# Low parts of the weights one use later, and a reordered projection stage in an NSA, S5 and mixed-attention kernel on one core

## The chip, the cores and the metric

One NeuronCore of a Trainium2 chip. The metric is the device time of one execution in microseconds (us), the median of the runs.

## The reference

A two-layer network on 512 tokens of width 1024, all in fp32. Layer 0 has a native-sparse-attention mixer and an S5 state-space mixer with a gated unit; the second block has a retention, a gated linear attention and a sliding-window attention, whose outputs are merged by gates; a feed-forward network ends it. Cut to what the change touches:

```python
def _compress(k, cmp_idx, pe, w1, w2):
    blk = k[:, cmp_idx] + pe[:, None, :]
    ...
    return jax.nn.silu(blk @ w1) @ w2

# mixer of layer 0: h @ w_in gives q, kc, vc, ks, vs, kw, vw, gates, z
k_cmp = _compress(kc, ...); v_cmp = _compress(vc, ...)      # 31 blocks of 32 tokens
s_c = einsum(q, k_cmp) - slopes * (t - cmp_center)
p_c = _masked_softmax(s_c, cmp_end <= t)                    # 16 heads
o = gate0 * (p_c @ v_cmp) + gate1 * selected + gate2 * window
# S5: state matrices from complex powers of 64-wide diagonals, applied in chunks
```

## The kernel before

The work is cut into tiles of 128 output columns by 512 tokens. Each fp32 product is three products of reduced-precision parts: hi times hi, hi times lo, lo times hi. So each weight piece (1024 columns by 128, 512 KB) goes through three steps: SyncE issues its load into one of 3 raw buffers, ScalarE copies it rounded to `whi` (L1249), VectorE subtracts to get `wlo` (L1720), both in a ring of 3. TensorE's `mm` (L822 to L824) uses one piece with the activations `Hh` and `Hl`, in 24 matmuls; `pair` (L842 to L844) runs two pieces side by side over the eight parts k of the activations, and waits for a piece's `wlo` at its first k and for `Hl` at each k, so that a norm still in the making paces it. `tok` (L861 to L863) has the weights move. There are 262 such pieces in the kernel.

The order is written once, by the class `Plan`: stages append steps to `self.order`, `with_weights` puts loads (`load`) and splits (`split`) in among them, and every engine walks the same list and does its own part of each step, in order. Waits are on semaphore counts. The piece that is `LOOK` = 2 uses ahead is split when a piece is first used. `tick()` puts a step of side work in between, which is `prep`: the state matrices of S5, made in the projection stage, in four rounds b. In each round `Bb` comes first, then the rotations CA (a power table `pw` times C, real and imaginary part) and W (`pr`, the table reversed, times `Bb`), six operations of half size each for one part; `prep_k` and `prep_wt` are matmuls that use them.

Before, VectorE does the real part of CA (`prep_ca`, 128x576), and POOL the imaginary one, its negation (`prep_neg`) and both parts of W. VectorE also makes the copies `Bd` of `Bb` (L1961) and, in `ev_kvc` (L1762), writes the tiles of w_kvc with the positional encoding added into `blk`. The compressed softmax (`cmp_soft`) works on a quarter of the queries and 16 heads after all eight score tiles. `Hl` is made at L1745 in the first norm, L1989 in the first block, L2326 before the feed-forward network; `total` (L874) sums squares over partitions.

The projection stage is `nsa`: squares of x, first norm, w_kvc in two pairs, the gate tile, cmp_w1 and cmp_out with tiles of w_q, six more tiles of w_q with scores, w_ksw with softmax, w_vsw, then the attention. `evict` gives a finished tile to the engine that copies it out.

```python
                if k == 0:
                    on.wait_ge(*before(plan.bank, key))
                    on.wait_ge(*at("wlo", i))
                on.wait_ge(*at("lo", src, k))
```

## Time and profile before

| | |
|---|---|
| median of 3 runs | 2047.48 us (2042.81 to 2052.18) |
| the profiled execution | 2053.18 us |
| its span, first to last instruction | 2051.4 us |
| TensorE busy | 1826.9 us, 89% |
| VectorE, ScalarE, POOL busy | 1005.5, 816.8, 303.3 us |
| mean granted clock of TensorE | 0.955 |

The span is cut by stage in what follows: 0 to 281 us the projection stage (with the S5 preparation), to 461 the attention, then the output projection w_o0, the S5 part, w_glu and w_o1, the second block from about 820 us, and the feed-forward network from 1640 us on. The granted clock is a share of full speed. Idle time in brackets names what ended it.

### The profile page before, as it was taken

The page shows a single profiled execution, that of the slowest core. Times are in us where ns is not written, and L with a number is a line of the kernel's source. Part 1 is how long each engine was busy: PE and PEld are TensorE (multiplying, and loading weights), DVE is VectorE, ACT ScalarE, POOL GpSimd, SP SyncE. Part 2 cuts the span into 40 slices and gives each one's busy share as a digit, 9 for nine tenths or more (in the row PEclk, how much of TensorE's full clock was granted, in tenths as well). Part 3 has the DMA queues.
Part 4 walks back from the last instruction along what each step waited for, and adds up shares of the span by engine and source line. Part 5 has one row for each costly group of instructions (what it writes and reads, how often), then busy time and mean ns, then how long its engine had stood idle before and what let it go on. Part 6 is the DMA issues. An engine that isn't in the chain of part 4 may idle for free.

```text
span 2051.4 us, 23580 instructions
## 1 busy us (share of the span) xinstructions
PE 1826.9 (89%) x9454; PEld 1450.1 (71%) x9454; DVE 1005.5 (49%) x1694; ACT 816.8 (40%) x1348; POOL 303.3 (15%) x376
## 2 busy tenths in 40 slices
PE   3488699997996999999799999999999969999996
PEld 2366578775775787786487777887777748888885
DVE  7647845665564446434434454445544364334323
ACT  4034356763313424333425545256632443223222
POOL 1347432546000000000000000012200021111000
PEclk9789799998998999999999999999999979999998
DMA  3154231005667422321032221321122212233231
GB/s 108 47 168 144 99 98 42 12 1 157 156 157 167 132 84 92 105 95 48 21 116 78 82 83 62 100 69 61 63 82 92 83 41 93 92 103 100 85 95 59
DMA packets 79230, 183.37 MB, mean 89 GB/s; under 512 B 24449, under 2 KB 35585, under 8 KB 77329
## 3 DMA queue, kind: packets, MB, share of 16 engines
q1 hardware_dynamic: 79120, 181.87, 28.7%
q8 instruction: 74, 1.21, 0.3%
q14 instruction: 36, 0.29, 0.0%
HBM read 165.58 MB, written 16.25 MB: 89 GB/s over the span
## 4 chain that ended last, share of the span: by engine, by line
PE 66%; DVE 17%; ACT 8%; DMA 4%; issue 2%; POOL 2%; SPq 1%; DVEq 0%; ACTq 0%; POOLq 0%
PE bank L822 16%; PE bank L823 16%; PE bank L824 15%; DVE wlo L1720 2%; PE bank L861 2%; PE bank L862 2%; PE bank L863 2%; PE bank L1003 2%; PE bank L981 2%; ACT whi L1249 1%; POOL Ps L2473 1%; ACT Ps L1619 1%; DVE Pb L1842 1%; DVE CA L1688 1%; PE bank L842 1%
## 5 line engine op out<-in xcount | busy, mean ns | idle before, releaser
L1720 DVE TENSOR_TENSOR wlo<-wraw,whi 128x1024 fp32r<-128x1024 f32 (+1 forms) x262 | 327.5, 1253 | 344.1 <-ACT whi L1249 342.7
L822 PE MATMUL bank<-Hh,whi 128*128 128x512 f32 (+2 forms) x1136 | 461.2, 406 | 24.0 <-DVE wlo L1720 13.2
L823 PE MATMUL bank<-Hl,whi 128*128 128x512 f32 (+2 forms) x1136 | 448.6, 395 | 0.0
L824 PE MATMUL bank<-Hh,wlo 128*128 128x512 f32 (+2 forms) x1136 | 448.2, 395 | 0.0
L1249 ACT ACTIVATE whi<-wraw 128x1024 fp32r<-128x1024 f32 (+1 forms) x262 | 271.1, 1040 | 373.0 <-PE bank L824 260.1
L822 PEld LDWEIGHTS bank<-Hh,whi 128*128 128x128 f32 (+2 forms) x1136 | 215.5, 190 | 84.5 <-DVE qs L1786 11.8
L824 PEld LDWEIGHTS bank<-Hh,wlo 128*128 128x128 f32 (+2 forms) x1136 | 215.3, 189 | 48.9 <-issue 0.6
L823 PEld LDWEIGHTS bank<-Hl,whi 128*128 128x128 f32 (+2 forms) x1136 | 215.8, 190 | 47.5 <-issue 2.7
L2466 POOL TENSOR_SCALAR bs<-dist 128x256 f32<-128x256 f32 x16 | 7.3, 457 | 831.8 <-DMA dist<-in_c_dist 831.1
L822 PE MATMUL bank<-Bh,whi 128*128 128x512 f32 x256 | 103.1, 403 | 2.2 <-DVE Bl L2244 2.2
L824 PE MATMUL bank<-Bh,wlo 128*128 128x512 f32 x256 | 102.1, 399 | 0.0
L823 PE MATMUL bank<-Bl,whi 128*128 128x512 f32 x256 | 101.9, 398 | 0.0
L1381 ACT ACTIVATE Pb<-Pb,stp 128x128 f32<-128x128 f32 (+3 forms) x128 | 70.8, 554 | 42.3 <-DVE stp L1842 41.5
L2428 POOL TENSOR_SCALAR Pb<-Pb,stp 128x128 f32<-128x128 f32 (+3 forms) x128 | 65.7, 532 | 100.7 <-DVE stp L1688 100.7
L1842 DVE CUSTOM_DVE_ANT_0 Pb<-bank,bias 128x128 f32<-128x128 f32 (+3 forms) x128 | 57.4, 487 | 33.1 <-PE bank L972 14.6
L842 PE MATMUL bank<-Hh,whi 128*128 128x512 f32 x80 | 36.3, 454 | 41.3 <-DVE Hl L2326 16.0
L861 PE MATMUL bank<-whi,Hh 128*128 128x512 f32 (+1 forms) x192 | 73.1, 381 | 0.0
L862 PE MATMUL bank<-whi,Hl 128*128 128x512 f32 (+1 forms) x192 | 72.6, 378 | 0.0
L863 PE MATMUL bank<-wlo,Hh 128*128 128x512 f32 (+1 forms) x192 | 72.5, 378 | 0.0
L822 PE MATMUL bank<-Fh,whi 128*128 128x512 f32 x176 | 69.8, 396 | 0.0
L823 PE MATMUL bank<-Fl,whi 128*128 128x512 f32 x176 | 69.8, 396 | 0.0
L824 PE MATMUL bank<-Fh,wlo 128*128 128x512 f32 x176 | 69.8, 396 | 0.0
(368 smaller groups left out, 3044.7 us busy)
## 6 DMA issues: line engine op xcount, KB each, us to landing
wraw<-in_w_o SPq DMA_DIRECT2D x24, 512.0 KB, 3.5
wraw<-in_w_bgate SPq DMA_DIRECT2D x24, 512.0 KB, 3.4
wraw<-in_w_branch SPq DMA_DIRECT2D x24, 512.0 KB, 3.5
wraw<-in_w_fg SPq DMA_DIRECT2D x22, 512.0 KB, 3.4
wraw<-in_w_fu SPq DMA_DIRECT2D x22, 512.0 KB, 3.4
wraw<-in_w_s SPq DMA_DIRECT2D x16, 512.0 KB, 4.1
wraw<-in_w_glu SPq DMA_DIRECT2D x16, 512.0 KB, 3.6
wraw<-in_w_fd SPq DMA_DIRECT2D x16, 512.0 KB, 3.5
```

Source lines behind the costliest of these rows:

```text
L822: pe.matmul(o, wh[:, cols], hi(k), start=k == 0, stop=False)
L823: pe.matmul(o, wh[:, cols], lo(k), start=False, stop=False)
L824: m = pe.matmul(o, wl[:, cols], hi(k), start=False, stop=k == K - 1)
L842: pe.matmul(o, wh[:, cols], hi(k), start=k == 0, stop=False)
L861: pe.matmul(o, hi(k)[:, rows], wh[:, cols], start=k == 0, stop=False)
L862: pe.matmul(o, lo(k)[:, rows], wh[:, cols], start=False, stop=False)
L863: m = pe.matmul(o, hi(k)[:, rows], wl[:, cols], start=False, stop=k == KT - 1)
L1249: return act.activation(o, i, ACT.Copy, **k)
L1381: x = act.activation(P[:, br, 0:W], P[:, br, 0:W], ACT.Exp, scale=-1.0, bias=s[:, n + br:n + br + 1], accum_out=s[:, 4 + n + br:5 + n + br])
L1720: dve.tensor_tensor(c.wlo[q][:, 0:n], c.raw[i % RR][:, 0:n], c.whi[q][:, 0:n].bitcast(F32), S_).then_inc(*up(DID, ("wlo", i)))
L1842: dve.tensor_tensor_reduce(out=P[:, br, 0:W], in0=bank(("s", u, m))[:, col:col + W], in1=bs[:, 512 - W:512], scale=1.0, scalar=3.0e38, op0 ...
L2428: gp.tensor_scalar(P[:, br, 0:W], P[:, br, 0:W], s[:, n:n + 1], 1.0, M, M).then_inc(*up(DID, ("pn", u + a, br)))
```

## The change

It does these things.

- In `with_weights` the high part stays where it was, two uses ahead. The low part becomes a step of its own, `split_lo`, and is put in at the first use of a piece: first the low part of the next piece, then the loads and the high part two ahead, then (if still open) its own. The raw buffer is free only after it. This holds for all 262 pieces of the kernel.
- The first norm: the table's small operations stand between the squares, the reciprocal root comes before the first three splits, and `norm0` makes `sq` of piece k+1 before `Hl` of k; low parts 0 to 2 come after all of it.
- The rotations run whole (128x1152, 128x1024) on VectorE, both parts, with the negation inside the last operation. POOL has only memsets and small copies in the stage.
- `Bd` copies and the tiles of w_kvc (`ev_kvc`) go to ScalarE; the positional encoding comes in as column 31 of `blk` and as a bias `hb` of the Silu.
- The compressed softmax runs per head index r (`soft_in`, `soft_out`), needs two score tiles, and has its mask in the bias and in `valid`.
- New tile order: one pair, then w_kvc 2 and 3 singly, gate, w_ksw with two cmp_w1 steps each, w_q in the order 0, 4, 1, 5, 2, 6, 3, 7, w_vsw. The stores of CA, K and W stand later. The wait for the last W store moves from POOL's `cmp_end` to ScalarE's first copies of the attention.

The core of the diff:

```diff
+        lows = deque()
+
+        def low(upto):
+            while lows and lows[0] <= upto:
+                i = lows.popleft()
+                out.append(("split_lo", i))
+                rawuser[i % RR] = -1
...
-                        rawuser[split % RR] = -1
+                        lows.append(split)
...
                     if i > seen:
                         seen = i
+                        low(i + 1)
                         pump(i + LOOK)
+                        low(i)
...
-            if k == 3:
-                self.tick(2)
+            if 1 <= k <= 6:
+                self.tick()
         self.step("consts")
         self.step("nsa_in")
+        self.inv("x", 0, 7, 0, 1.0 / D, "rs")
+        self.tick()
         self.step("pump")
-        self.inv("x", 0, 7, 0, 1.0 / D, "rs")
-        self.tick(3)
...
+        for n in range(2, 4):
+            self.filled("w_kvc", n, 3)
+        self.filled("w_gate", 0, 3, M=48)
         for t in range(4):
-            self.filled("w_ksw", t)
...
+            for hf in range(2):
+                j = self.piece("cmp_w1", (i, m, hf), 0, 1024, split=False)
+                self.step("cmp_w1", i, m, hf, j)
+                self.tick()
...
+        for n, t in enumerate(self.turns):
+            self.filled("w_q", t, 1)
+            if n == 0:
+                self.cmp_out(1)
+            self.compressed(n)
...
+    def rotated(o, x, w, n, y, i, b, step, *names):
...
+        if step == 0:
+            tt(o, yk(0), wk(i), M)
+        elif step == 1:
+            tt(x, yk(1), wk(1 - i), M)
+        else:
+            tt(o, o, x, A_ if i else S_, *names)
...
+        if (i, n) == (1, 2):
+            on.wait_ge(*now(DID))
+            dve.scalar_tensor_tensor(o, o, -1.0, x, M, S_).then_inc(*up(DID, ("CA", b)))
...
-    def prep_ca(b, n):
-        if n == 0:
-            on.wait_ge(*at("Cq", b))
-            on.wait_ge(*at("Bb", b))
...
-        rot(*c.rotate(c.tG, c.pw, 9, c.Cq, 1, c.CA[:, 1, :, :, :], b, n), *([("CA_im", b)] if n == 5 else []))
```

How the instructions stand, at three places. In the rows a name with a number is a buffer of a ring (wlo_57 to wlo_59 are the three low parts, wraw and whi the raw and high parts, sqb squares, nacc their sum).

VectorE before the w_s5 pair, in the kernel before; the pair uses wlo_58 and wlo_59:

```order
L1729 TENSOR_TENSOR nacc_67<-nacc_67,sqb_65 128x512
L1720 TENSOR_TENSOR wlo_59<-wraw_52,whi_56 128x1024
L1983 TENSOR_TENSOR X<-X,bank 128x512
L1989 SCALAR_TENSOR_TENSOR Hl<-X,vecs,Hh 128x512
L1729 TENSOR_TENSOR nacc_67<-nacc_67,sqb_66 128x512
L1994 TENSOR_TENSOR vecs<-vecs 128x8
L1995 MEMSET D_142 128x8
L1997 MEMSET Xs_151 128x16
L1997 MEMSET Xs_152 128x16
L1720 TENSOR_TENSOR wlo_57<-wraw_53,whi_54 128x1024
```

and with the change:

```order
L1769 TENSOR_TENSOR wlo_58<-wraw_51,whi_55 128x1024
L2029 TENSOR_TENSOR X<-X,bank 128x512
L2035 SCALAR_TENSOR_TENSOR Hl<-X,vecs,Hh 128x512
L1778 TENSOR_TENSOR nacc_67<-nacc_67,sqb_66 128x512
L2040 TENSOR_TENSOR vecs<-vecs 128x8
L2041 MEMSET D_140 128x8
L2043 MEMSET Xs_149 128x16
L2043 MEMSET Xs_150 128x16
L1769 TENSOR_TENSOR wlo_59<-wraw_52,whi_56 128x1024
L1769 TENSOR_TENSOR wlo_57<-wraw_53,whi_54 128x1024
```

The low part of the pair's second piece, wlo_59, stood eight rows higher, before the last tile's X, Hl and nacc; it stands behind them, beside that of the following piece.

VectorE before the w_fg/w_fu pair, whose norm is the rows X and Hl (ft and Fl are the feed-forward network's activations), before:

```order
L2315 SCALAR_TENSOR_TENSOR mg<-mg,vecs,rs 128x512
L2321 TENSOR_TENSOR X<-X,mg 128x512
L2326 SCALAR_TENSOR_TENSOR Hl<-X,vecs,Hh 128x512
L2321 TENSOR_TENSOR X<-X,mg 128x512
L2326 SCALAR_TENSOR_TENSOR Hl<-X,vecs,Hh 128x512
L1720 TENSOR_TENSOR wlo_58<-wraw_51,whi_55 128x1024
L2338 TENSOR_TENSOR ft_215<-bank,rs 128x512
L2341 TENSOR_TENSOR ft_215<-ft_215,bank 128x512
L2343 TENSOR_TENSOR Fl<-ft_215,Fh 128x512
L1720 TENSOR_TENSOR wlo_59<-wraw_52,whi_56 128x1024
```

and with the change:

```order
L2361 SCALAR_TENSOR_TENSOR mg<-mg,vecs,rs 128x512
L2367 TENSOR_TENSOR X<-X,mg 128x512
L2372 SCALAR_TENSOR_TENSOR Hl<-X,vecs,Hh 128x512
L2367 TENSOR_TENSOR X<-X,mg 128x512
L2372 SCALAR_TENSOR_TENSOR Hl<-X,vecs,Hh 128x512
L1769 TENSOR_TENSOR wlo_57<-wraw_53,whi_54 128x1024
L1769 TENSOR_TENSOR wlo_58<-wraw_51,whi_55 128x1024
L2384 TENSOR_TENSOR ft_213<-bank,rs 128x512
L2387 TENSOR_TENSOR ft_213<-ft_213,bank 128x512
L2389 TENSOR_TENSOR Fl<-ft_213,Fh 128x512
L1769 TENSOR_TENSOR wlo_59<-wraw_52,whi_56 128x1024
L1769 TENSOR_TENSOR wlo_57<-wraw_53,whi_54 128x1024
```

The pair's second low part is wlo_57, behind the last Hl; before, it stood ahead of the norm's first row.

VectorE in the first norm, around the first three low parts; before:

```order
L1729 TENSOR_TENSOR nacc_67<-nacc_67,sqb_65 128x512
L1733 MEMSET ones 128x128
L1734 MEMSET epst 128x1
L1735 MEMSET epst 128x1
L1720 TENSOR_TENSOR wlo_57<-wraw_51,whi_54 128x1024
L1720 TENSOR_TENSOR wlo_58<-wraw_52,whi_55 128x1024
L1720 TENSOR_TENSOR wlo_59<-wraw_53,whi_56 128x1024
L1688 TENSOR_TENSOR sm<-pw 128x32 x2
L1688 TENSOR_TENSOR pw<-sm 128x32
L1688 TENSOR_TENSOR sm<-pw 128x32 x2
```

and with the change:

```order
L1797 TENSOR_TENSOR Hl<-sq_64,Hh 128x512
L1792 SCALAR_TENSOR_TENSOR sq_64<-X,vecs,rs 128x512
L1797 TENSOR_TENSOR Hl<-sq_63,Hh 128x512
L1797 TENSOR_TENSOR Hl<-sq_64,Hh 128x512
L1769 TENSOR_TENSOR wlo_57<-wraw_51,whi_54 128x1024
L1769 TENSOR_TENSOR wlo_58<-wraw_52,whi_55 128x1024
L1769 TENSOR_TENSOR wlo_59<-wraw_53,whi_56 128x1024
```

They stood right behind the squares; they stand behind the last Hl, and before Hl the next piece's `sq` has its place.

## Rows read from the trace of the kernel before

**Rows 1.** the page, part 1, busy time of each engine

```profile
PE 1826.9 (89%) x9454; PEld 1450.1 (71%) x9454; DVE 1005.5 (49%) x1694; ACT 816.8 (40%) x1348; POOL 303.3 (15%) x376
```

**Rows 2.** windows of core 0 (columns: us, then each engine's busy us, clock, DMA share, GB/s)

```profile
0.00:281.00 281.00, 185.46 (x933) 146.12 (x934) 181.72 (x310) 91.44 (x141) 117.78 (x86) 0.87 0.35 116
281.00:461.00 180.00, 172.76 (x1355) 135.59 (x1355) 109.58 (x390) 123.53 (x336) 74.96 (x144) 0.99 0.08 25
461.00:2051.00 1590.00, 1468.63 (x7174) 1168.38 (x7170) 714.25 (x994) 601.85 (x871) 110.54 (x147) 0.97 0.30 92
...
220.00:240.00 20.00, 8.72 (x43) 7.20 (x43) 18.50 (x24) 7.11 (x12) 17.02 (x13) 0.76 0.18 53
```

**Rows 3.** waits of TensorE: us in total, times, longest

```profile
PE bank L822 <- DVE wlo L1720: 30.4, 7, 15.3
PE bank L905 <- DMA wraw<-in_cmp_w: 21.1, 1, 21.1
PE bank L1040 <- DMA mW<-scratch_W: 20.0, 2, 15.5
PE bank L842 <- DVE Hl L2326: 16.0, 7, 6.4
PE bank L951 <- DVE sC L1688: 15.3, 2, 11.3
PE bank L842 <- DVE wlo L1720: 13.6, 1, 13.6
```

**Rows 4.** timeline, start of the norm, first pair, attention (start us, us, instruction, [idle before])

```profile
28.65 0.74 DVE L1743 SCALAR_TENSOR_TENSOR sq<-X,vecs,rs 128x512 f32<-128x512 f32 x1
28.88 0.77 PE L842 MATMUL bank<-Hh,whi 128*128 128x512 f32 x1 [10.21 <-DVE Hl L1745]
...
30.10 0.69 DVE L1745 TENSOR_TENSOR Hl<-sq,Hh 128x512 fp32r<-128x512 f32 x1 [0.70 <-ACT Hh L1249]
...
281.20 0.29 DVE L1842 CUSTOM_DVE_ANT_0 Pb<-bank,bias 128x128 f32<-128x128 f32 x1 [7.28 <-POOL bias L2417]
```

**Rows 5.** groups of VectorE by line, 0 to 281 us

```profile
L1720 DVE TENSOR_TENSOR wlo<-wraw,whi 128x1024 fp32r<-128x1024 f32 (+1 forms) x23 | 34.8, 1524 | 34.9 <-ACT whi L1249 34.8
L1961 DVE COPY Bd<-Bb 64x128 f32<-64x128 f32 x16 | 16.7, 1043 | 0.3
```

**Rows 6.** timeline of VectorE, rotations beside POOL and without it

```profile
92.77 1.58 DVE L1688 TENSOR_TENSOR CA<-Cq,pw 128x576 f32<-128x576 f32 x1
...
242.31 0.76 DVE L1688 TENSOR_TENSOR CA<-Cq,pw 128x576 f32<-128x576 f32 x1
```

**Rows 7.** timeline of TensorE, restart in w_o0

```profile
493.82 0.79 PE L822 MATMUL bank<-qs,whi 128*128 128x512 f32 x1 [15.28 <-DVE wlo L1720]
...
495.26 0.63 PE L822 MATMUL bank<-qs,whi 128*128 128x512 f32 x1
495.69 0.63 PE L823 MATMUL bank<-zsr,whi 128*128 128x512 f32 x1
```

**Rows 8.** timelines of TensorE and VectorE, w_s5

```profile
523.36 0.39 PE L842 MATMUL bank<-Hh,whi 128*128 128x512 f32 x1
...
527.47 0.11 DVE L1997 MEMSET Xs<- 128x16 f32 x2
...
560.58 0.39 PE L822 MATMUL bank<-Hh,whi 128*128 128x512 f32 x1
...
565.53 0.68 DVE L1688 TENSOR_TENSOR Xs<-Xs,xt 128x504 f32<-128x504 f32 x1
```

**Rows 9.** timelines of TensorE and VectorE, gated linear attention, head 1

```profile
1143.17 0.39 PE L822 MATMUL bank<-Hh,whi 128*128 128x512 f32 x1
...
1147.21 0.69 DVE L1688 TENSOR_TENSOR gk<-gk,gt 128x512 f32<-128x512 f32 x1
```

**Rows 10.** timelines of VectorE and TensorE, w_fg/w_fu pair

```profile
1669.20 0.75 DVE L2326 SCALAR_TENSOR_TENSOR Hl<-X,vecs,Hh 128x512 fp32r<-128x512 f32 x1 [0.79 <-ACT Hh L1249]
...
1671.92 1.02 PE L874 MATMUL bank<-nacc,ones 128*128 128x512 f32 x2
```

More of the change, by code:

```diff
@@ L277, in nsa @@
             self.step("norm0", k)
-            self.sq.give(("n0", k))
-        for i in range(2):
-            keys = [("w_kvc", 2 * i), ("w_kvc", 2 * i + 1)]
-            self.pair(keys, "h0")
-            for key in keys:
-                self.evict(key)
-            self.tick(4)
-        self.filled("w_gate", 0, M=48)
-        self.bank.take("gateT")
-        self.step("gate_t")
-        self.bank.give("gateT")
-        for i in range(2):
-            self.bank.take(("hid", i))
-            for m in range(2):
-                for hf in range(2):
-                    j = self.piece("cmp_w1", (i, m, hf), 0, 1024, split=False)
-                    self.step("cmp_w1", i, m, hf, j)
-                    self.tick()
-            self.step("cmp_hid", i)
-            self.bank.give(("hid", i))
-            if i:
-                self.step("cmp_in")
-            self.filled("w_q", i)
-            self.bank.take(("cmp", i))
-            self.step("cmp_out", i)
-            self.bank.give(("cmp", i))
@@ L304, in nsa @@
-        for t in range(2, 8):
-            self.filled("w_q", t)
-            self.cmp_scores(t - 2)
-        for t in range(4):
-            self.filled("w_ksw", t)
-            if t < 2:
-                self.cmp_scores(6 + t)
-            if t >= 1:
-                self.cmp_softmax(t - 1)
+            if k < KT:
+                self.sq.give(("n0", k))
+        self.pair([("w_kvc", 0), ("w_kvc", 1)], "h0")
+        for n in range(2):
+            self.evict(("w_kvc", n))
+        self.tick(2)
@@ L432, in prep @@
     def prep(self):
-        for part in range(11):
+        for part in range(9):
             self.step("prep", part)
@@ L454, in prep @@
             self.bank.give(("kk", b))
-            yield
-            for n in range(6):
+            for n in range(3):
                 self.step("prep_w", b, 1, n)
+                if n == 2:
+                    self.step("store_k", b)
                 yield
-            self.prep_turn(b, 0)
-            yield
-        self.prep_turn(3, 1)
+        self.prep_turn(3, 0)
+        self.step("store_w", 3, 0)
     def prep_turn(self, b, i):
@@ L990, in nd @@
             on.wait_ge(*before(plan.bank, ("o", t)))
-            for n in range(4):
-                on.wait_ge(*at("pcT", n))
+            on.wait_ge(*at("pcT", r))
             for a in range(2):
@@ L1296, in norm0 @@
     def norm0(k):
+        if k == KT:
+            return
         on.wait_ge(*at("n0", k))
@@ L1714, in cmp_end, with split_lo @@
         c.ev.stand(("cmp_end",), DID)
-    def split(i):
+    def split_lo(i):
         n = plan.pieces[i][3]
@@ L2343, in ffn @@
         dve.tensor_tensor(lo(k), s, hi(k).bitcast(F32), S_).then_inc(*up(DID, ("lo", "f", k)))
-    evict = {"w_kvc": ev_kvc, "w_q": ev_q, "w_ksw": ev_ksw, "w_o0": ev_o0, "w_s5": ev_s5, "w_o1": ev_o1, "w_r": ev_r,
+    evict = {"w_q": ev_q, "w_ksw": ev_ksw, "w_o0": ev_o0, "w_s5": ev_s5, "w_o1": ev_o1, "w_r": ev_r,
              "w_rg": ev_gates, "w_gg": ev_gates, "w_ga": ev_ga, "w_g": ev_g, "w_bgate": ev_bgate, "w_branch": ev_branch,
@@ L2391, in nsa_in, with prep @@
             gp.memset(c.kl[o:o + 64, :, :, a, :].bitcast(F32), 0.0).then_inc(*up(DID, *([("kl0",)] if a else [])))
+        gp.memset(c.Bd[:, :, :, :], 0.0).then_inc(*up(DID, ("Bd0",)))
+        on.wait_ge(*at("cmp_pe"))
+        on.wait_ge(*now(DID))
+        for i in range(2):
+            gp.tensor_copy(c.blk[i][:, :, 31], c.pe2[:, i, :]).then_inc(*up(DID, ("blk_pe", i)))
+        on.wait_ge(*at("total", "x"))
+        gp.memset(c.Kp[:, :, 0:8, :], 0.0).then_inc(*up(DID, ("Kp0",)))
+    def prep(part):
+        if part == 5:
+            on.wait_ge(*at("pw"))
+            for k in range(8):
+                x = gp.tensor_copy(c.pr[:, :, k, :], c.pw[:, :, 7 - k, :])
+            x.then_inc(*up(DID, ("pr",)))
     def prep_r(m):
@@ L2524, in consts @@
         get(c.vecs[:, 0:12, :], I["vecs"], "vecs")
+        get(c.valid, I["c_valid"], "valid")
         get(c.ident[:, :], I["c_ident"], "ident")
```

389 lines of the change are left out of this document (200 added, 189 removed).

## The prediction, made before the change was run

> **What bounds the kernel now.** I read the page first, then the windows, the waits of TensorE, and for each disputed place the timeline of TensorE beside VectorE's. The page [rows 1] has PE busy for 1826.9 of the span's 2051.4 us, so 224.5 us are its idle time, and nothing that takes work off the other engines helps unless one of those idle stretches shrinks. The windows [rows 2] say where they lie: 95.5 us in the first 281 us, the projection stage, where the clock's mean is only 0.87; 7 us in the attention; 121 us in the 1590 us after it. VectorE is busy 181.7 us of the stage's 281 and POOL 117.8, and both stand before PE there. The waits [rows 3] name what ends last: low parts of weights (wlo), a DMA of cmp_w, Hl of the norm, and sC of the softmax.
>
> So the change has two accounts: the projection stage, which it rebuilds, and the 1770 us behind it, where only one thing changes, the place of the low parts on VectorE.
>
> **Account 1, the projection stage.**
> Prologue. 24 small VectorE operations now stand among the squares (about 0.22 us each with their pitch, 5.3 us), and the reciprocal root comes before the weights' high parts, which ScalarE then makes ahead of Hh. Where the last square's sum lets PE total it at 16.6 now, I get about 23, with 1.5 us lost in the alternation, and rs near 28. The norm's pitch per piece is 2.05 us now (sq 0.74, 0.70 waiting, Hl 0.69 [rows 4]); pipelined it is the two operations, 1.38 a piece. Hl of piece 7 then ends at about 41.3, but the first pair also needs the low parts behind it, some 1.2 us each: its first piece starts at about 42.5 in place of 28.88 [rows 4], where it was paced by Hl and done soon after the norm, at 44. Now 48 matmuls run without waiting, 11 us at 0.23 and 1.4 for a slow start (see below), to about 55. Cost: 11 us.
> Rotations. VectorE's halves take some 1.6 us beside POOL's and 0.76 when POOL is idle [rows 6]. Whole, at twice the elements, I take 1.39 for 128x1152 (less than twice 0.76, since each operation has a fixed part) and 1.25 for 128x1024. Per b that is 2.0 (Bb) + 6 x 1.39 + 6 x 1.25 = 17.8 us, against 15.8 on VectorE now (2.0, 6 x 1.6, and 4.2 for Bd [rows 5], which goes to ScalarE). But POOL's 12 halves and the negation, some 20 us per b, are gone, and the low parts return from the stage's mean of 1.52 us [rows 5] to about 1.2.
> What PE then sees. Blk evictions leave VectorE, the softmax loses its mask product and its transposes wait for two tiles instead of eight (most of PE's 15.3 us of waits on sC [rows 3] goes), and cmp_w's 21.1 us DMA wait [rows 3] goes, since those pieces are loaded between ksw tiles. Walking the new order with these durations: second pair's work split over two tiles, done at 71 (today it is done there too); gate 77; ksw tiles 84, 98, 112, 125, each with its two cmp_w1 pieces and a wait of 2 to 3 us for ScalarE's kh copies and high part; q tiles at 6.9 us to 190; vsw to 212; then PE waits for VectorE's rotations of b = 3 (to 228) and the last transposes (237). Attention's first VectorE operation moves from 281.2 [rows 4] to about 242. Gain: 39 us. The bounds: 60, if the ksw rounds and the b = 3 tail don't wait (VectorE's sum then sets about 220); 20, if each wide operation delays a low part or an eviction by half its length in front of a tile.
>
> **Account 2, low parts one use later.** A low part is 1.2 us on VectorE. At steady tiles (5.5 us each) it makes no difference whether it runs one or two tiles ahead: VectorE waits for the high part today anyway. The difference is where a stage turns. There the step is a pair, or a tile behind a long VectorE chain; the low part used to stand ahead of the chain and now stands behind it. I went through all 262 pieces: take the end of the VectorE work that now precedes the low part, add 1.2, and compare with PE's start on that piece. Five were late before, nineteen are now. The terms:
> - w_o0's second tiles: the chain ends 500.6, PE wanted the piece at 493.82, where it already came out of 15.28 idle [rows 7]. Part is hidden; 4 us.
> - w_s5's pair: order shows the low part behind nacc, D and both Xs. VectorE ends those at 527.6 [rows 8]; the pair's first matmul is at 523.36 without a gap [rows 8], and its second piece's first three follow at 524.0. 528.7 - 524.0 = 4.7, plus 1.4 for the slow restart: 6.1.
> - inside S5: three pieces wait behind the scan chain that ends at 566.2 (PE wanted one at 560.58 [rows 8]; late by 6.8), the others by 5.8 and 6.9; and one by 8. The waits on mW, 20.0 us [rows 3], absorb most; 10 of 27 remain.
> - w_glu's pair behind two Yl (7.2) and a tile before it (2.1): 9.
> - w_o1's pair behind zyr 778.4 (4.2) and its fourth tile, already a late one, by 6.0, of which 4 is new, with 1.8 for restarts: 10.
> - w_r's pair and second pair, 4.7 and 4.1, with restarts: 9.4.
> - retention, three pieces by 2.4 to 3.3, two under existing waits for ro: 4.
> - gated linear attention: in heads 1 to 3 two pieces each; the first by 3.4; behind gk, which ends at 1147.9, the second, which PE wanted at 1143.17 with no idle there [rows 9], by 5.8 in all, less 1.1 of idle that exists: 4.7 each, 14.1; head 0 3.6, the way out 2.8: 20.5.
> - sliding window's ends, 1.8 and the like: 4.5.
> - w_fg/w_fu pair: here the eight Hl pace the pair (16.0 us of waits in 7 [rows 3]), so its 48 matmuls lie inside the norm and are done at 1671.92 [rows 10]. With the second piece's low part behind Hl 7 (ends 1669.95) all but three of them start at 1671.2 and take 10.2 us and 1.4 of slow clock: 1682.8. 11.
> Sum 88.5 us. A restart costs the slow clock's 0.43 us a matmul instead of 0.23 for about the first seven ([rows 7]: from 493.82 on), 1.4 us. The bounds are 45, if waits behind each site (DMA, norm chains) swallow half, and 110, if the 15 places where I counted no restart have one.
> The other engines: SP's stores stand a little later and loads come one use later; a load takes 3.5 us, a use 5.5, and only POOL's old wait on W stores had that on the path, which the change moves. Nothing.
>
> **Sum.** 2053.2 - 39 + 88.5 = 2102.7 by the profiled execution, which is 5.7 above the median of the runs; on the median 2047.5 + 50 = 2097. 0.5% of this kernel is 10 us, about what a measurement can tell from no change.
>
> **A rule against a row.** Operations of 128x1152 occupy VectorE twice as long at a stretch as the halves do. The rows have halves of 0.76 and, beside POOL, about 1.6 [rows 6], so by the rows a late low part waits no longer than it does today. The Trainium skill (Perfetto Trace Analysis, Optimizing Scalar/DVE Operations) says that where VectorE is not saturated but makes bubbles elsewhere, breaking instructions up gets work done sooner. By it the merging would cost in the stage, to the end that rival 3 gives.
>
> **The rivals.**
> 1. Faster. The stage gains 60, since VectorE without POOL beside it keeps up, and the late low parts are absorbed by slack further on, at most 25 us left: 2047.5 - 60 + 25 = 2012 at best, about 2030 in the middle. It decides when the loss of account 2 is under the gain, so below 39 us. For it: 121 us of idle behind attention can swallow lateness, and VectorE no longer blocks on the high parts (its waits before them are long in today's trace). Against: at the nineteen places I counted, PE has little or no idle time of its own now [rows 8, 9]. 0.12.
> 2. Even. Gain and loss near 45 each: 2047. 0.11.
> 3. Stage without gain. Wide operations (48 of 1.25 to 1.39 us), ScalarE's added copies (16 per kvc tile) and the later prologue give the 39 back: each of 24 wide operations in front of a low part costs 0.7 more, 17 us, and b = 3's tail 20. Then 2047.5 - 39 + 88.5 + 37 = 2134. For: at 220 to 240 PE is busy only 8.7 of 20 while VectorE is at 18.5 [rows 2], so VectorE bounds there. 0.12.
> 4. The change does not do what it says for the low parts, or PE waits by another order than I read (hi parts late, so low parts would have been as late before): then only the stage counts, 2008. 0.03.
> The forecast itself, a net loss of 25 to 75, has the rest, 0.62.
>
> **Range and chances.** From the bounds: 60 gained and 60 lost gives 2047; 20 gained and 100 lost gives 2128. I take 2042 to 2134; the forecast's own range is 2072 to 2122. Faster by over 0.5%: 0.15 (rivals 1 and 4); within: 0.11 (rival 2); slower: 0.74 (forecast and rival 3).
>
> **What would show it.** In the profile after: the first attention operation (bias product on VectorE) near 242; PE's waits on wlo, now 44 us in 8 waits [rows 3], near 110 us in some 20; a gap of about 25 us behind the first three matmuls of the w_fg/w_fu pair, then 45 in a row; a gap of 5 us before w_s5's pair; VectorE's rotations at about 1.4 us, POOL idle up to 235. If wlo waits sum to under 60, account 2 fails; if attention starts after 270, account 1 does; if both hold and the time is below 2070, waits for other things shrank by as much, and mW, U and ro are where to look.

## The result, and the profile after

The changed kernel takes 2090.25 us (median of 4 runs, 2088.4 to 2091.07), the kernel before 2047.57: 1.0207 times as long, interval 1.0183 to 1.0232, so 42.7 us slower. The forecast was 2097.

The page of the changed kernel, its span and part 1 [rows 1]:

```profile
span 2088.6 us, 23526 instructions
PE 1839.0 (88%) x9454; PEld 1460.6 (70%) x9454; DVE 969.9 (46%) x1629; ACT 833.4 (40%) x1400; POOL 197.2 (9%) x312
```

TensorE has 12 us more busy time for the same 9454 matmuls (its mean granted clock is 0.946 where it was 0.955) and 25 us more idle time (249.6 against 224.5). These are sums of a stage that gains and a rest that loses. From w_o0's first matmul to the end, TensorE is busy 1494.5 us against 1468.6 [rows 2], at a granted clock of 0.94 against 0.97, so of the 84 us more there some 26 are slower matmuls and some 58 idle time:

```profile
414.30:2088.00 1673.70, 1494.48 (x7166) 1186.22 (x7164) 704.36 (x995) 601.72 (x871) 108.15 (x147) 0.94 0.28 88
```

Over the whole span VectorE is busy 36 us less and POOL 106 us less: the time does not follow the busy time of the two engines that were relieved.

Where the time went shows in the start of each stage's first matmul, read from the timelines of TensorE in both kernels. All of these steps issue the same matmuls in both, so they can be laid side by side:

| stretch | before | after | difference | forecast |
|---|---|---|---|---|
| start to w_o0's first matmul | 461.4 | 414.3 | -47.1 | -39 |
| w_o0, to w_s5's pair | 62.0 | 66.7 | +4.7 | +4 |
| S5, to w_glu's pair | 161.3 | 177.2 | +15.9 | +16.1 |
| w_glu, to w_o1 | 90.0 | 99.0 | +9.0 | +9 |
| w_o1, to w_r | 48.6 | 58.5 | +9.9 | +10 |
| w_r and retention | 200.1 | 216.2 | +16.1 | +13.4 |
| gated linear attention | 266.5 | 288.8 | +22.3 | +20.5 |
| sliding window | 213.1 | 206.4 | -6.7 | +4.5 |
| merge, norm, w_fg/w_fu pair | 168.9 | 181.9 | +13.0 | +11 |
| rest of the feed-forward network | 379.5 | 379.6 | +0.1 | 0 |

The sum is 37.2 us, the difference of the two spans; the forecasts sum to 49.5. By the medians the kernel is 42.7 us slower, since the profiled execution of the kernel before was 5.7 us above its median and that of the changed kernel was at its median. Every line from w_o0 to the feed-forward pair has places where a low part comes late; in the sliding window's something else outweighs them (e5). The first line holds the attention too, and it also changed: 180.2 us before, 175.8 after (last section). The waits of TensorE in the changed kernel (us in total, times, longest), against [rows 3]:

```profile
PE bank L844 <- DVE wlo L1769: 102.0, 27, 14.9
PE bank L864 <- DVE wlo L1769: 66.1, 7, 25.7
PE bank L1037 <- DVE CA L2008: 11.3, 1, 11.3
PE bank L1132 <- ACT ro L1269: 8.0, 1, 8.0
PE bank L864 <- DVE Hl L2372: 6.4, 1, 6.4
```

Waits on wlo were 44.0 us in 8 and are 168.1 in 34. Behind w_o0's start alone they were 27.6 in 6 and are 137.0 in 28. The waits on cmp_w (21.1, in the projection stage) and on mW (20.0, in S5) are gone, Hl before the feed-forward network went from 16.0 to 6.4. A wait that comes first hides those that would have come after it, so behind w_o0 the 109 us more on wlo are 84 us more of time.

Three of the places in the timelines. First w_s5's pair [rows 8] (VectorE, then TensorE):

```profile
484.98 1.20 DVE L1769 TENSOR_TENSOR wlo<-wraw,whi 128x1024 fp32r<-128x1024 f32 x1
486.11 1.22 DVE L1769 TENSOR_TENSOR wlo<-wraw,whi 128x1024 fp32r<-128x1024 f32 x1
...
486.24 0.79 PE L864 MATMUL bank<-Hh,whi 128*128 128x512 f32 x1 [4.38 <-DVE wlo L1769]
```

The low part of the pair's second piece starts at 484.98, beside the last small operations on Xs; three matmuls of the first piece have run from 481.02 on, and the pair resumes at 486.24, after 4.38 us. The row at 486.11 is already the following piece's. Then the feed-forward pair [rows 10]:

```profile
1693.26 0.75 DVE L2372 SCALAR_TENSOR_TENSOR Hl<-X,vecs,Hh 128x512 fp32r<-128x512 f32 x1 [0.79 <-ACT Hh L1269]
1693.82 1.31 POOL L2522 TENSOR_TENSOR nacc<-nacc,sqb 128x512 f32<-128x512 f32 x1 [1.90 <-ACT sqb L1301]
1693.93 2.29 DVE L1769 TENSOR_TENSOR wlo<-wraw,whi 128x1024 fp32r<-128x1024 f32 x1
...
1696.37 0.77 PE L864 MATMUL bank<-Hh,whi 128*128 128x512 f32 x1 [25.66 <-DVE wlo L1769]
```

Hl 7 ends at 1694.0, then comes the pair's own low part; at 1696.37 TensorE has stood 25.66 us. In the kernel before, 45 of the pair's 48 matmuls were issued in that stretch of the norm. The low part takes 2.29 us here and not some 1.2: POOL's operation began 0.11 us before it and ended at 1695.13, 1.09 us before it did (see Contention below). And gated linear attention [rows 9], where TensorE had no wait on a low part before (only three of about 1 us on gt):

```profile
1103.88 0.61 PE L844 MATMUL bank<-Hh,whi 128*128 128x512 f32 x1 [2.29 <-DVE wlo L1769]
1156.68 0.50 PE L844 MATMUL bank<-Hh,whi 128*128 128x512 f32 x1 [3.21 <-DVE wlo L1769]
1164.67 0.50 PE L844 MATMUL bank<-Hh,whi 128*128 128x512 f32 x1 [2.23 <-DVE wlo L1769]
```

### The profile page after: what moved, and what is told of

The parts are those of the page before. It is cut to its first block, busy times and chain, and to the rows that moved or that the text cites. A ratio compares the mean times of both kernels' runs of the same rounds, so it can differ in the third digit from the quotient of the medians.

```text
span 2088.6 us, 23526 instructions
## 1 busy us (share of the span) xinstructions
PE 1839.0 (88%) x9454; PEld 1460.6 (70%) x9454; DVE 969.9 (46%) x1629; ACT 833.4 (40%) x1400; POOL 197.2 (9%) x312
## 4 chain that ended last, share of the span: by engine, by line
PE 77%; DVE 14%; ACT 6%; issue 2%; DMA 1%; SPq 1%; POOL 0%; DVEq 0%; ACTq 0%
PE bank L844 19%; PE bank L846 18%; PE bank L845 18%; DVE wlo L1769 2%; PE bank L883 2%; PE bank L885 2%; PE bank L884 2%; PE bank L1024 2%; PE bank L1003 1%; PE bank L864 1%; PE bank L865 1%; PE bank L866 1%; DVE Pb L1879 1%; PE bank L993 1%; DMA X<-in_xT 1%
## 5 line engine op out<-in xcount | busy, mean ns | idle before, releaser
L844 PE MATMUL bank<-Hh,whi 128*128 128x512 f32 (+1 forms) x1152 | 477.3, 414 | 73.6 <-DVE wlo L1769 73.6
L845 PE MATMUL bank<-Hl,whi 128*128 128x512 f32 (+1 forms) x1152 | 462.5, 401 | 0.0
L846 PE MATMUL bank<-Hh,wlo 128*128 128x512 f32 (+1 forms) x1152 | 461.7, 401 | 0.0
L1769 DVE TENSOR_TENSOR wlo<-wraw,whi 128x1024 fp32r<-128x1024 f32 (+1 forms) x262 | 316.8, 1226 | 85.3 <-ACT whi L1269 85.2
L844 PEld LDWEIGHTS bank<-Hh,whi 128*128 128x128 f32 (+1 forms) x1152 | 223.1, 194 | 140.8 <-DVE wlo L1769 64.8
L846 PEld LDWEIGHTS bank<-Hh,wlo 128*128 128x128 f32 (+1 forms) x1152 | 222.8, 193 | 51.7 <-issue 0.9
L845 PEld LDWEIGHTS bank<-Hl,whi 128*128 128x128 f32 (+1 forms) x1152 | 224.0, 194 | 49.9 <-issue 2.9
L864 PE MATMUL bank<-Hh,whi 128*128 128x512 f32 x64 | 29.0, 453 | 59.3 <-DVE wlo L1769 52.9
L1778 DVE TENSOR_TENSOR nacc<-nacc,sqb 128x512 f32<-128x512 f32 x42 | 31.7, 769 | 98.8 <-ACT sqb L1301 98.8
```

Of the source, the lines that this page charges most:

```text
L844: pe.matmul(o, wh[:, cols], hi(k), start=k == 0, stop=False)
L845: pe.matmul(o, wh[:, cols], lo(k), start=False, stop=False)
L846: m = pe.matmul(o, wl[:, cols], hi(k), start=False, stop=k == K - 1)
L864: pe.matmul(o, wh[:, cols], hi(k), start=k == 0, stop=False)
L1769: dve.tensor_tensor(c.wlo[q][:, 0:n], c.raw[i % RR][:, 0:n], c.whi[q][:, 0:n].bitcast(F32), S_).then_inc(*up(DID, ("wlo", i)))
```

## The experiments

Each was compared with the kernel before, run in the same session on the same chip. Ratios are given where they say more than the medians, since the kernel before itself had medians from 2046.0 to 2049.7 us in the four sessions (e1 to e4, e5 to e8, e9 to e11, e12). Starts and waits are those of one profiled execution of each. e2 and e10 are edits to the kernel before, e3 and e4 to the changed kernel, e5 to e9 and e11 to e1, and e12 to e9. A diff shows the lines that matter; `...` stands for lines left out.

**e1_low_at_split.** The changed kernel, with the low parts back behind the high parts:

```diff
-                        lows.append(split)
+                        out.append(("split_lo", split))
+                        rawuser[split % RR] = -1
```

> The changed kernel with every low part right behind its high part again (two uses ahead, raw buffer free then), all else as changed. Theory A, the late low parts cause the loss behind the attention and the projection stage's gain does not need them: w_o0 starts near 414 us as in the changed kernel (461 before), the rest takes the 1590 us of before, about 2047.5 - 47 = 2000 us (1995 to 2012), and TensorE's waits on wlo fall from 168 us to under 60. Rival B, the loss behind the attention has another cause (stores and loads standing elsewhere, buffers): above 2060 us. Rival C, the stage's gain comes from the late low parts: w_o0 starts after 435 us, 2020 us or more.

Measured: 1997.84 us, ratio 0.9746 (0.9727 to 0.9766). w_o0 starts at 410.5, and from there to the end of the span it takes 1585.7 us (before 1590.0, with the change 1674.3). Its waits:

```profile
PE bank L845 <- DVE wlo L1770: 34.6, 11, 15.3
PE bank L1061 <- DMA mW<-scratch_W: 18.7, 3, 14.5
PE bank L865 <- DVE Hl L2373: 15.0, 7, 6.4
PE bank L1038 <- DVE CA L2009: 13.7, 1, 13.7
PE bank L1228 <- DVE ss L2335: 7.4, 7, 1.7
```

Theory A holds to 3 us: the sign of the whole change hangs on the place of one kind of instruction. mW and ss stand in the list again, as before the change. B and C are out. Against e1 the late low parts of the changed kernel cost 8.3 us up to the attention's first operation (238.5 against 230.2), give back 4.5 in the attention (175.8 against 180.3) and cost 88.6 behind it.

**e2_before_low_late.** The kernel before, with the `low` functions of the change and nothing else of it:

```diff
-                        rawuser[split % RR] = -1
+                        lows.append(split)
...
+                        low(i + 1)
                         pump(i + LOOK)
+                        low(i)
```

> The kernel before with only the low parts (and the raw buffers' release) one use later. Theory A: the loss behind the attention comes whole, 1671 us in place of 1590 from w_o0's start, and the stage changes little: 2047.5 + 81 = 2128 us (2115 to 2140). Rival B, the placement alone does little: 2040 to 2065 us. Rival C, late low parts help the stage since VectorE no longer stands before whi: w_o0 starts 15 us or more earlier than 461, so below 2113 us.

Measured: 2132.83 us, ratio 1.0416 (1.0391 to 1.0441). w_o0 starts at 464.3 and the rest takes 1674.6 us, where the changed kernel takes 1674.3; stretch by stretch the two differ by 0.2 us at most.

```profile
PE bank L831 <- DVE wlo L1729: 100.8, 28, 14.9
PE bank L851 <- DVE wlo L1729: 83.8, 8, 25.6
PE bank L914 <- DMA wraw<-in_cmp_w: 20.8, 1, 20.8
```

So the loss does not need the rebuilt stage: 84.6 us behind w_o0's start here, 88.6 between e1 and the changed kernel. The 4 us between these are e1's, whose rest is 4.2 us shorter than before, mostly in S5 and the retention; why was not looked into. By the medians e2 costs 83 us; its profiled execution was 7.9 us above its median. Late low parts gain nothing in the projection stage (C): the attention's first operation comes 6.0 us later, and the attention is 3.1 us shorter, so w_o0 starts 2.9 us later.

**e3_late_in_stage_only.** Late for the first 29 pieces only.

```diff
+        STAGE = 29
...
-                        lows.append(split)
+                        if split < STAGE:
+                            lows.append(split)
+                        else:
+                            out.append(("split_lo", split))
+                            rawuser[split % RR] = -1
```

> The changed kernel, with low parts late for the pieces of the projection stage only (the first 29) and right behind the high part from w_z0 on. Theory A: as e1 within 6 us, about 2000 us, w_o0 starts near 414. Rival C: at least 15 us faster than e1. If e1 is the faster one by over 6 us, late low parts cost in the stage too.

Measured: 2008.33 us, 10.5 slower than e1 in the same session. It comes from the start of the program; TensorE's first pair, in e3 and in e1:

```profile
42.30 0.80 PE L870 MATMUL bank<-Hh,whi 128*128 128x512 f32 x1 [18.42 <-DVE wlo L1775]
```

```profile
35.20 0.77 PE L865 MATMUL bank<-Hh,whi 128*128 128x512 f32 x1 [10.70 <-DVE Hl L1798]
```

With the low parts behind the eight Hl the pair cannot be paced by the norm: it starts 7.1 us later, and w_o0 8.3 us later. The forecast's prologue term (11 us for the whole prologue) was of this kind.

**e4_one_piece_early.** The changed kernel with one of the 262 low parts put back, the second piece of the feed-forward pair.

```diff
-                        lows.append(split)
+                        if split == 203:
+                            out.append(("split_lo", split))
+                            rawuser[split % RR] = -1
+                        else:
+                            lows.append(split)
```

> The changed kernel with one low part of 262, that of the second piece of the w_fg/w_fu pair, back behind its high part, ahead of the norm. Theory A: the wait of 25.7 us splits into seven short ones on Hl, the pair is done inside the norm, 12 to 13 us earlier: 2090.3 - 12.5 = 2078 us. Rival D, what comes next is late anyway (the 5.1 us wait on wlo behind Fl grows): 2086 us or more.

Measured: 2077.02 us, 13.2 less than the changed kernel's 2090.25 (in another session; ratios 1.0129 and 1.0207). The waits on both kinds in the pair:

```profile
PE bank L868 <- DVE wlo L1773: 40.4, 6, 18.4
PE bank L868 <- DVE Hl L2376: 13.9, 7, 6.4
```

The wait of 25.7 us is gone from the first line (66.1 in 7 in the changed kernel), and the second is 13.9 in 7 where it was 6.4 in 1. Theory A again, and the next low part (behind Fl) took nothing back.

**e5_late_in_swa_only.** e1, with low parts late for pieces 162 to 178.

```diff
-                        out.append(("split_lo", split))
-                        rawuser[split % RR] = -1
+                        if 162 <= split <= 178:
+                            lows.append(split)
+                        else:
+                            out.append(("split_lo", split))
+                            rawuser[split % RR] = -1
```

> As e1_low_at_split (1997.8 us), but low parts one use later for pieces 162 to 178, those beside the sliding-window attention. Theory: there VectorE's wait of 3.2 us for whi ahead of wlo delays the softmax row sums that TensorE waits for (ss, 7.2 us in 7 waits before, none in the changed kernel), so late is better here and only here: 1.5 to 8 us faster, about 1991 us, and the ss waits go. Rival: the 6.7 us that the changed kernel gained in this stretch came from elsewhere: 1998 us, ss waits stay.

Measured: 1985.93 us, ratio 0.9693 (0.9654 to 0.9732). The stretch of the sliding window takes 201.4 us, in e1 212.7, before 213.1, with the change 206.4; no wait on ss is left. The reason stands in VectorE's timeline, before:

```profile
1431.64 0.23 DVE L1692 TENSOR_SCALAR ss<-ss,sink 128x4 f32<-128x4 f32 x1
1435.05 1.23 DVE L1720 TENSOR_TENSOR wlo<-wraw,whi 128x1024 fp32r<-128x1024 f32 x1 [3.18 <-ACT whi L1249]
```

and with the change:

```profile
1459.17 0.23 DVE L1741 TENSOR_SCALAR ss<-ss,sink 128x4 f32<-128x4 f32 x1
1459.31 1.22 DVE L1769 TENSOR_TENSOR wlo<-wraw,whi 128x1024 fp32r<-128x1024 f32 x1
```

Before, the low part of the piece two uses ahead stood 3.18 us for whi, which ScalarE can write only when TensorE is done with the ring's slot, and the softmax rows behind it stood too. One use later, whi is long there. The end pieces of the stretch are early again in e5, which accounts for most of the other 5 us (in the changed kernel TensorE waits 2.65 and 1.62 us for wlo there). Of the stretches behind w_o0 this is the one in which late is better; in front of it the attention is another (last section).

**e6_prologue_as_before.** e1, with the splits ahead of the reciprocal root again.

```diff
-            if 1 <= k <= 6:
-                self.tick()
+            if k == 3:
+                self.tick(2)
         self.step("consts")
         self.step("nsa_in")
-        self.inv("x", 0, 7, 0, 1.0 / D, "rs")
-        self.tick()
         self.step("pump")
+        self.inv("x", 0, 7, 0, 1.0 / D, "rs")
...
+        self.tick(5)
         self.pair([("w_kvc", 0), ("w_kvc", 1)], "h0")
```

> As e1_low_at_split, but the prologue's order of before: high and low parts 0 to 2 ahead of the reciprocal root, two prep parts after the fourth square, the rest after the norm; the pipelined norm stays. Theory: first pair starts near 29 us in place of 35.2, so 4 to 7 us faster, about 1992 us. Rival: the prep parts moved behind the norm only push VectorE's rotations later, which end the stage: within 2 us of e1.

Measured: 1993.66 us, ratio 0.9734 (0.9703 to 0.9765): by time not told from e1. In the profiled executions the first pair starts at 25.93 instead of 35.20, and w_o0 5.4 us earlier; 4 of the 9 us went into a longer wait for wlo ahead of the next tile (6.87 against 2.79). That is in between the two expectations. The `tick(5)` puts the side work that stood among the squares behind the norm.

**e7_rotations_on_pool.** e1, with the rotations divided over VectorE and POOL as in the kernel before (`rotate` and `rot` as there, in halves). The first piece below is VectorE's, the second POOL's for i = 1; `prep_w` goes there likewise for both i.

```diff
     def prep_ca(b, i, n):
...
+        if i == 0:
+            for st in (2 * n, 2 * n + 1):
+                (o, a0, a1, op) = c.rotate(c.tA[:, 0:4], c.pw, 9, c.Cq, 0, c.CA[:, 0, :, :, :], b, st)
+                tt(o, a0, a1, op, *([("CA_re", b)] if st == 5 else []))
...
+    def prep_ca(b, i, n):
+        if i == 0:
+            return
...
+        for st in (2 * n, 2 * n + 1):
+            rot(*c.rotate(c.tA[:, 4:8], c.pw, 9, c.Cq, 1, c.CA[:, 1, :, :, :], b, st))
```

> As e1_low_at_split, but the rotations split as before: real part of CA in halves on VectorE, imaginary part, its negation and W in halves on POOL. Theory A, the two engines get in each other's way (halves of 1.5 to 1.8 us in place of 0.76, low parts of 1.5 to 2.1 us in place of 1.2) and POOL's some 30 us a round become the chain: attention starts 8 to 25 us later, 2006 to 2023 us. Rival B: the last round's 16 us in a row on VectorE run in parallel, up to 5 us faster, 1993 us; the stage's gain then was from the order alone.

Measured: 2002.05 us, ratio 0.9781 (0.9752 to 0.981): 0.35% more than e1, about 7 us, the intervals overlapping; w_o0 starts 3.1 us later (the other 4 us of its span come behind w_o0, where the edit changes nothing). VectorE's groups in the first 260 us:

```profile
L1771 DVE TENSOR_TENSOR wlo<-wraw,whi 128x1024 fp32r<-128x1024 f32 (+1 forms) x26 | 36.5, 1412 | 45.7 <-ACT whi L1271 45.5
L1739 DVE TENSOR_TENSOR CA<-Cq,pw 128x576 f32<-128x576 f32 x8 | 12.1, 1513 | 0.6
```

The halves are at 1.51 us and the low parts at 1.41 again, in e1 1.36 for a whole operation and 1.20. So the contention of the two engines came back, but nearly all of its price was hidden. Moving the rotations, the largest part of the change by busy time, is worth some 3 us of the 51 that e1 gains up to w_o0.

**e8_bd_on_vector.** e1, with the `Bd` copies in VectorE's `prep_b`.

```diff
...
-                x = copy(c.Bd[half, i, :, h * 16:h * 16 + 16], c.Bb[half, i, :, :])
+                x = dve.tensor_copy(c.Bd[half, i, :, h * 16:h * 16 + 16], c.Bb[half, i, :, :])
```

> As e1_low_at_split, but the four Bd copies per round back on VectorE. With POOL idle they should take about 0.35 us each and not 1.04: 1.4 us a round, of which only the last round's is on the path: 1998 to 2001 us. Rival: they take 1.04 us each (4.2 a round) whatever POOL does: 2002 to 2010 us.

Measured: 1991.6 us, ratio 0.9731 (0.9701 to 0.976), by time the same as e1; w_o0 starts 8.3 us earlier. The copies:

```profile
L1983 DVE COPY Bd<-Bb 64x128 f32<-64x128 f32 x16 | 3.5, 222 | 0.3
```

222 ns each with POOL idle; they were 1043 ns [rows 5] when POOL was rotating. ScalarE takes 308 ns for one and has to come to it in its own order. Both expectations were too slow. By the ratios e8 is 0.15% faster than e1, some 3 us, with the intervals overlapping; its profiled execution, at 1989.1 us, was the fastest of its four. That the stage edits are worth what the profiles say shows in e9.

**e9_all_but_ticks.** The edits of e5, e6 and e8 together, as their diffs have them.

> e1_low_at_split with what the runs since showed put together: Bd copies on VectorE, low parts late for pieces 162 to 178 only, the prologue's order of before. If the parts add (about 8, 7 and 5 us in the profiled executions): w_o0 starts near 398 to 403 us, end 1975 to 1983 us. If the prologue's and Bd's gains both only shorten VectorE's chain up to the last round, they don't add: 1984 to 1988 us.

Measured: 1971.73 us, ratio 0.9625 (0.9604 to 0.9645). w_o0 starts at 398.5, 12 us before e1's, of 13.7 that the two stage edits gave alone. They add nearly whole, and the ratios bear it out: e9 is 0.68% faster than e5, 14 us.

**e10_before_ksw_between.** The kernel before with a w_ksw tile behind each two cmp_w1 steps.

```diff
                     self.step("cmp_w1", i, m, hf, j)
                     self.tick()
+                self.filled("w_ksw", 2 * i + m)
...
-            self.filled("w_ksw", t)
```

> The kernel before with one part of the new tile order: a w_ksw tile behind every two cmp_w1 steps, none left at the end; softmax and rotations as before. Theory: TensorE's 21.1 us wait for cmp_w's load falls under 8 us, but the softmax of a quarter of the queries has no tiles left to hide behind, and its waits (sC, 15.3 us before) grow by as much: 2040 to 2060 us. Rival: the order alone brings the stage's gain: under 2030 us.

Measured: 2045.05 us, ratio 0.9988 (0.9975 to 1.0002): no difference. The wait for cmp_w's load, 21.1 us, is gone. In its place:

```profile
99.90 0.80 PE L822 MATMUL bank<-Hh,whi 128*128 128x512 f32 x1 [17.76 <-DVE wlo L1720]
139.34 0.79 PE L822 MATMUL bank<-Hh,whi 128*128 128x512 f32 x1 [9.72 <-DVE wlo L1720]
```

The waits for wlo ahead of two of those tiles are 17.8 and 9.7 us; the softmax's did not grow (sC went from 15.3 to 11.6). The number came as expected and the reason did not: in VectorE's timeline the low part that TensorE waits for at 99.90 stands behind blk evictions, Bd copies and six rotations of one round, from 75 to 97.6 us. The order alone brings nothing. Which relief of VectorE it needs was not tried; by e7 it is not that of the rotations.

**e11_more_ticks.** e1, with one more step of side work per w_q tile.

```diff
-            self.filled("w_q", t, 1)
+            self.filled("w_q", t, 2)
```

> e1_low_at_split with two steps of preparation per w_q tile in place of one, so that the last round's rotations stand earlier. Theory: the 13.7 us wait for CA behind the vsw tiles shrinks to under 5 us, 6 to 12 us faster: 1985 to 1991 us. Rival: VectorE is full at 160 to 200 us (88% and 78% busy), and the waits only move to qs and wlo: within 3 us of e1.

Measured: 1994.54 us, ratio 0.9736 (0.9716 to 0.9756), within 2 to 3 us of e1. The wait for CA, 13.7 us in e1, is split:

```profile
207.20 1.94 PE L1038 MATMUL bank<-CA,Bd 128*32 128x128 f32 x32 [1.13 <-DVE CA L2009]
214.06 1.94 PE L1048 MATMUL bank<-ident,WT 128*128 128x128 f32 x8 [4.92 <-DVE WT L1738]
```

w_o0 starts 4.4 us earlier; new waits on qs (4.26 and 1.26) took part of the 7.7 us. Again between theory and rival by the profile; by time not told from e1.

**e12_all.** e9 with the edit of e11.

> e9_all_but_ticks (1971.7 us, w_o0 at 398.5) with two steps of preparation per w_q tile as in e11. If the tail's wait for CA (12.3 us) shrinks as it did there (to 1.1 and 4.9 us on WT): 4 to 6 us faster, 1966 to 1968 us. Rival: with the prologue's order of before the preparation starts later, so that the extra ticks only crowd the q tiles (waits on qs): within 2 us of e9.

Measured: 1971.91 us, ratio 0.9629 (0.9609 to 0.965): the same as e9. In the profiled execution (1976.9 us, 5 above the median) w_o0 starts 2.5 us earlier, and w_o0 and S5 take 7.6 us more. The longest wait of w_o0 ends at the same time in both, in e12 and in e9:

```profile
428.49 0.80 PE L848 MATMUL bank<-qs,whi 128*128 128x512 f32 x1 [15.28 <-DVE wlo L1762]
```

```profile
428.92 0.80 PE L848 MATMUL bank<-qs,whi 128*128 128x512 f32 x1 [13.26 <-DVE wlo L1762]
```

VectorE's timelines show what stands behind it. X of w_o0's first tile comes ahead of that low part, and it waits for a load, in e12 and in e9:

```profile
414.58 0.69 DVE L2031 TENSOR_TENSOR X<-X,bank 128x512 f32<-128x512 f32 x1 [14.67 <-DMA X<-in_xT]
...
425.46 2.98 DVE L1762 TENSOR_TENSOR wlo<-wraw,whi 128x1024 fp32r<-128x1024 f32 x1
```

```profile
416.23 0.69 DVE L2031 TENSOR_TENSOR X<-X,bank 128x512 f32<-128x512 f32 x1 [13.87 <-DMA X<-in_xT]
...
425.51 3.36 DVE L1762 TENSOR_TENSOR wlo<-wraw,whi 128x1024 fp32r<-128x1024 f32 x1
```

The load lands 1.65 us earlier in e12. From there to the end of the low part VectorE takes 13.9 us, in e9 12.6: its Hl, Hl, nacc and low part take 1.75, 2.66, 2.78 and 2.98 us (1.22, 2.04, 2.33 and 3.36 in e9), while POOL works without a break on operations of up to 2.9 us. Apart from POOL they take some 0.75, 0.75, 0.7 and 1.2. The kernel before, the changed kernel and e1 show the same row of events; no run moved the load or POOL's work.

## Why the prediction was right

**The two accounts.** It was right to take the change apart by reach: a stage that is rebuilt, and one line that acts on the whole kernel. e1 and e2 show both apart: w_o0 starts 51 us earlier by the stage without late low parts, and late low parts cost 85 to 89 us behind w_o0. The total was 12 us better than forecast in the profiled executions (37.2 against 49.5): 11.2 of it is the sliding window's term, 4.4 the attention, which had none, and 3.7 the stage; the other terms were 7 short.

**Account 2.** Forecast 88.5, measured 84.3 behind w_o0's start, and by the table each term is within 3 us but one. (The tile before w_glu's pair is in w_glu's forecast and in S5's stretch; the two together are 25.1 forecast, 24.9 measured.) The steps were the end of the VectorE work now ahead of the low part, 1.2 us, and TensorE's start on the piece before. Two sizes were too small at the feed-forward pair, 11 against 13.0: the low part took 2.29 us beside POOL and not 1.2, and after the 25.66 us of idle TensorE issued twelve matmuls 0.43 us apart (the granted clock is 0.50 from 1696.4 to 1701, the lower of its two levels) where the forecast had seven, so that the restart cost some 2.4 us and not 1.4. The term that failed is "sliding window's ends, 1.8 and the like: 4.5". The 1.6 and 2.7 us at its ends are there, but the stretch is 6.7 us shorter. I had written that "at steady tiles it makes no difference ... VectorE waits for the high part today anyway". That is the error: the wait stands in VectorE's queue, and whoever is behind it pays. I had [rows 3]'s smaller waits in the same view (ss, 7.2 us in 7) and did not ask what stood ahead of ss. e5 measured it at 11 us. The same error hides a second gain: by the forecast's own division the attention belongs to this account, it had no term, and the late low parts make it 3 to 4.5 us shorter (last section). With it the account is 79.9 against 88.5.

**Account 1.** Forecast 39, measured 42.7 at the attention's first operation (281.20 to 238.52; forecast 242). Steps that the trace of after bears out:

```profile
42.23 0.80 PE L864 MATMUL bank<-Hh,whi 128*128 128x512 f32 x1 [18.43 <-DVE wlo L1769]
...
214.83 1.36 DVE L1737 TENSOR_TENSOR CA<-Cq,pw 128x1152 f32<-128x1152 f32 x1
221.79 1.36 DVE L2008 SCALAR_TENSOR_TENSOR CA<-CA,tA 128x1152 f32<-128x1152 f32 x1
...
223.29 2.10 PE L1037 MATMUL bank<-CA,Bd 128*32 128x128 f32 x17 [11.25 <-DVE CA L2008]
...
238.52 0.29 DVE L1879 CUSTOM_DVE_ANT_0 Pb<-bank,bias 128x128 f32<-128x128 f32 x1 [6.54 <-POOL bias L2478]
```

The first pair at 42.23 (42.5), the rotations at 1.36 us (1.39; 128x1024 at 1.23, forecast 1.25), the wait of TensorE for the last round's CA (11.25 at 223), and the four ksw rounds with 2.0 to 2.7 us each (2 to 3). The number came out near, for a partly wrong reason: here luck had a share. I put much of the stage's gain down to rotations without POOL beside them; e7 says 3 us of it are that. e8 says the Bd copies moved to ScalarE cost 8 of it (by the profiled executions), where I had booked 4.2 us a round as gained on VectorE. e10 says the tile order alone gives none. Some 48 of e1's 51 us remain without the rotations. They are left to the new order, the softmax per head index, the blk evictions on ScalarE and the new prologue together; these were not tried apart, so the cause of the stage's gain is not shown.

**The check on waits.** I had forecast "near 110 us in some 20"; it was 168 in 34. I counted differences in arrival and not whole waits: a late low part ends a wait that began as another's (mW, Hl, ss), and takes its full length into its own line. As a sign of right or wrong the number was badly built.

**The rivals.** Faster (1): w_o0 started 47 us earlier, and the loss was 84 and not under 39; e4 shows one site alone at 13. Even (2): out, the ratio's interval is 1.0183 to 1.0232. Stage without gain (3): out; whether the wide operations hold low parts up more than halves would, no run here separates, since the steps of a tick stand together either way. The Trainium skill (Perfetto Trace Analysis, Optimizing Scalar/DVE Operations) says that breaking instructions up may allow work to be completed sooner where an unsaturated engine makes others wait; halves beside POOL in e7 were 3 us slower, and halves on VectorE alone were not run. Rival 4 (the place of the low part changes nothing): out by e2.

**Contention.** The rows of e7 and e8 bear out what [rows 6] had. With POOL at work a VectorE operation of two SBUF inputs takes 1.51 us instead of 0.76, and a 64x128 copy 1043 ns in the mean instead of 222. The mean of the copies hides what happens. The four of a round in the kernel before, the first of them alone, and POOL's operations beside them:

```profile
83.17 0.22 DVE L1961 COPY Bd<-Bb 64x128 f32<-64x128 f32 x1
83.17 4.18 DVE L1961 COPY Bd<-Bb 64x128 f32<-64x128 f32 x4
```

```profile
83.28 1.22 POOL L2433 TENSOR_TENSOR CA<-Cq,pw 128x576 f32<-128x576 f32 x1 [75.11 <-DVE Bb L1688]
84.58 1.22 POOL L2433 TENSOR_TENSOR tG<-Cq,pw 128x576 f32<-128x576 f32 x1
85.87 1.40 POOL L2433 TENSOR_TENSOR CA<-CA,tG 128x576 f32<-128x576 f32 x1
```

The first copy began 0.11 us before POOL and took 0.22 us. The other three took 1.18, 1.28 and 1.46 us and ended at 84.58, 85.87 and 87.35, each 0.08 us after one of POOL's operations; it is so in all four rounds, to 0.01 us. Each copy waited out one operation of POOL. The low part of the feed-forward pair above did the same: POOL's operation had 1.20 us left when it began, and it took 1.1 us longer than alone. The Trainium skill (SBUF — State Buffer, Who interferes with whom) calls this an exclusive lock on a port pair that the two engines share, and says of VectorE's two-port modes, which copies can enter, that whoever issues first gets the pair for the whole instruction. The trace agrees for the copies to 0.1 us. What moving the rotations did to VectorE is measured: up to the attention it is busy 157.8 us in e1 and 140.3 in e7, and yet the stage of e1 is 3.2 us shorter.

## What to carry to other kernels

When a producer is moved in an in-order queue, list the places where its consumer has no slack, not the mean distance: here most of 262 low parts did not mind, some 22 more that TensorE waits for cost 84 us behind w_o0 (28 waits in place of 6), and two lines put right gave 4.4% (2090 to 1998). And look at what the moved instruction waits for as well as at who waits for it: early is right where a stage turns, late is right where the instruction would stand in its queue for an operand that cannot be there yet. A schedule with both (e9: late only beside the sliding window, with the stage edits of e6 and e8) gave 1971.7 us, 3.75% under the kernel before. Low parts late in the attention too were not tried on top of it. And price a busy engine's relief by the number of its operations that stand beside the other engine's, not by their size alone.

## What the runs showed that I had not expected

A plain 64x128 fp32 copy on VectorE was slowed 4.7 times in the mean by POOL's work (1043 against 222 ns), the two-input operations only twice (1.51 against 0.76, [rows 6]). In microseconds both paid about the same, 0.8 in the mean, and the rows above say why: an operation waits out what is left of one of POOL's, however short it is itself. So the Bd copies, 16.7 us in the stage [rows 5], were 3.5 us of work.

And the attention itself became 4.4 us shorter (175.8 us from its first VectorE operation to w_o0, before 180.2) though its code hardly changed. The window of the changed kernel shows the same busy time on VectorE and ScalarE as [rows 2], within 1 us:

```profile
238.00:414.00 176.00, 170.51 (x1361) 135.02 (x1360) 109.72 (x390) 124.08 (x336) 78.14 (x144) 1.00 0.08 25
```

The runs tell what goes with it. Where the low parts are late in the attention it takes 175.8 (the changed kernel), 175.9 (e4) and 177.1 us (e2); where they are early, 180.2 (before, e10), 180.3 (e1) and 179.9 to 180.2 (e5 to e9). VectorE's timeline has the reason that e5 has for the sliding window. Before, all eight low parts of the attention's first 76 us stood 1.7 to 5.2 us for whi; with the change none did. The third, before and with the change:

```profile
300.69 1.23 DVE L1720 TENSOR_TENSOR wlo<-wraw,whi 128x1024 fp32r<-128x1024 f32 x1 [5.24 <-ACT whi L1249]
```

```profile
251.87 1.22 DVE L1769 TENSOR_TENSOR wlo<-wraw,whi 128x1024 fp32r<-128x1024 f32 x1
```

It is not the whole of it: in e3, e11 and e12, with early low parts there, the attention takes 178.5 to 178.7 us, and what shortened it in these was not looked into.
